# Second block on an unscaled residual, gates as token rows, scan sums by accumulating transfers, a one-matmul bucket row, aligned buffers

## What is computed

```python
h = rms_norm_2(x, norm_w)
q, k, v, a_gate, u, z, g_a, g_s = split(h @ w_in)
attn = sliding_window_attention(rms(q), rms(k), v, sinks)
y_a = (attn * silu(a_gate)) @ w_attn_proj
y_ssm = gelu(s5_ssm(u, ...))          # s[t] = a * s[t-1] + b[t], complex, 4096 states
glu_a, glu_b = split(y_ssm @ w_glu + b_glu)
y_s = (glu_a * sigmoid(glu_b) * silu(z)) @ w_ssm_proj
merged = sigmoid(g_a) * y_a + sigmoid(g_s) * y_s
out = x + merged @ w_out
```

## Time and profile before

| | us |
|---|---|
| median of three runs | 3322.17 |
| profiled execution, its own time | 3322.21 |
| its span, first to last instruction | 3320.3 |
| PE busy / PEld busy | 3140.2 / 2725.1 |
| DVE busy / ACT busy / POOL busy | 2021.3 / 1538.3 / 59.3 |
| mean granted clock | 0.983 |

### The profile page before, as it was taken

How to read it: one execution, slowest core, us unless ns; L and a number is a source line. 1 busy time by engine, 2 the same in 40 slices (tenths; PEclk the granted TensorE clock), 3 DMA queues, 4 the chain that set the end, 5 groups by cost and what they waited for, 6 DMA issues and landing times.

```text
span 3320.3 us, 47412 instructions
## 1 busy us (share of the span) xinstructions
PE 3140.2 (95%) x17370; PEld 2725.1 (82%) x17370; DVE 2021.3 (61%) x2350; ACT 1538.3 (46%) x1975; POOL 59.3 (2%) x99
## 2 busy tenths in 40 slices
PE   8999898999999998989989999999997998999999
PEld 7798777888888887987877888888885888989997
DVE  5567755555555555676655555555556557888664
ACT  5554545544444444545455444444444455544443
POOL 0000000000000000000000000000001000000000
PEclk9999999999999999999999999999998999999999
DMA  6645363655555555544554555555553433444555
GB/s 238 221 167 175 134 211 119 207 189 188 190 187 189 187 189 171 178 147 152 180 169 154 196 184 190 189 190 189 184 189 114 164 111 129 156 146 153 169 178 180
DMA packets 159835, 577.01 MB, mean 174 GB/s; under 512 B 17504, under 2 KB 20240, under 8 KB 158544
## 3 DMA queue, kind: packets, MB, share of 16 engines
q1 hardware_dynamic: 151936, 549.52, 49.6%
q10 hardware_dynamic: 5616, 13.51, 1.2%
q0 software_dynamic: 2144, 12.02, 1.0%
HBM read 568.43 MB, written 6.55 MB: 173 GB/s over the span
## 4 chain that ended last, share of the span: by engine, by line
PE 74%; DVE 11%; ACT 5%; issue 4%; DVEq 3%; DMA 1%; ACTq 1%; POOL 1%; POOLq 0%; SPq 0%
PE acc L624 19%; PE acc L626 19%; PE acc L625 19%; PE acc L632 4%; PE acc L634 4%; PE acc L635 4%; DVE lo L1482 3%; PE tp L643 1%; DVE sr L2098 1%; ACT hi L1020 1%; PE tp L676 1%; ACT lg L1102 1%; DVEq L2076 0%; PE tp L774 0%; ACT ze L1353 0%
## 5 line engine op out<-in xcount | busy, mean ns | idle before, releaser
L1482 DVE TENSOR_TENSOR lo<-raw,hi 128x1024 fp32r<-128x1024 f32 x1040 | 1263.4, 1223 | 943.5 <-ACT hi L1020 934.7
L1020 ACT ACTIVATE hi<-raw 128x1024 fp32r<-128x1024 f32 x1040 | 1093.9, 1058 | 1273.6 <-PE acc L626 970.4
L624 PE MATMUL acc<-hi,xh 128*128 128x512 f32 (+2 forms) x2272 | 883.8, 389 | 6.7 <-DVE lo L1482 3.7
L625 PE MATMUL acc<-lo,xh 128*128 128x512 f32 (+2 forms) x2272 | 875.8, 385 | 0.0
L626 PE MATMUL acc<-hi,xl 128*128 128x512 f32 (+2 forms) x2272 | 875.5, 385 | 0.0
L632 PE MATMUL acc<-xh,hi 128*128 128x256 f32 x1664 | 487.3, 293 | 35.9 <-DVE lo L1482 35.5
L624 PEld LDWEIGHTS acc<-hi,xh 128*128 128x128 f32 x2272 | 428.5, 189 | 94.7 <-issue 6.6
L626 PEld LDWEIGHTS acc<-hi,xl 128*128 128x128 f32 x2272 | 428.4, 189 | 85.1
L625 PEld LDWEIGHTS acc<-lo,xh 128*128 128x128 f32 x2272 | 428.7, 189 | 82.5
L634 PE MATMUL acc<-xl,hi 128*128 128x256 f32 x1664 | 476.3, 286 | 0.0
L635 PE MATMUL acc<-xh,lo 128*128 128x256 f32 x1664 | 476.0, 286 | 0.0
(11 more groups left out here) (366 smaller groups left out, 2629.8 us busy)
## 6 DMA issues: line engine op xcount, KB each, us to landing
raw<-in_stream SPq DMA_DIRECT2D x1040, 512.0 KB, 3.4
gpost<-in_post_g POOLq DMA_DIRECT2D x6, 1024.0 KB, 5.1
bpad<-in_b_pad ACTq DMA_DIRECT2D x8, 512.0 KB, 5.1
row<-in_rows POOLq DMA_DIRECT2D x3, 896.0 KB, 8.7
toep_scratch<-toep ACTq DMA_DIRECT2D x1, 2304.0 KB, 7.9
y<-in_mem SPq DMA_DIRECT2D x4, 512.0 KB, 8.4
h<-in_x ACTq DMA_DIRECT2D x4, 512.0 KB, 5.8
mem_scratch<-memkv ACTq DMA_DIRECT2D x1, 2048.0 KB, 6.6
```

Of the source, the lines that this page charges most:

```text
L624: nc.tensor.matmul(o, ah, hi[s][:, k, 0:g.width], start=first, stop=False)
L625: nc.tensor.matmul(o, ah, lo[s][:, k, 0:g.width], start=False, stop=False)
L1020: nc.scalar.activation(hi[s][:, :, :], raw[s][:, :, :], ACT.Copy).then_inc(hi_done, 1)
L1482: nc.vector.tensor_tensor(lo[s][:, :, :], raw[s][:, :, :], hi[s][:, :, :].bitcast(F32), ALU.subtract).then_inc(split_done, 1)
```

## The change

- **Bucket row.** One matmul (`relt` as weights, 12 rows by 384) is done before the first product; ACT copies the 12x384 result and one transfer writes it to memory 128 times over. The six turns in mem_k1 are gone. The second and the fourth transposes of the memory rows move ahead, ACT's and DVE's splits of unit 0 stand ahead of the first `xh`, and a one-column copy by ACT stands first of all. The step-size arithmetic of DVE and the keys of the second layer change places.
- **Aligned buffers.** `sb` starts at a multiple of 512 and rounds sizes to 64, so that every buffer starts on a multiple of 64 bytes.
- **Unscaled residual in the second block.** `raw_norm` takes the place of `norm`. q, kv and the gates are scaled by `rs` as ACT reads them; u, ag and z by `rsb2` (the row of `rs` on all partitions) as DVE reads them, with ACT's Silu after it on SBUF.
- **Token rows.** ga, ap, gs and sp are in form T (96 units). The merged rows stand in `y`, and PE transposes them in four turns `mix0` to `mix3` before the groups out.
- **Scan sums.** `back` and `forward` no longer add: DVE writes the four products of each into `sds` and `srs`, and POOL issues a transfer of 128x2048 elements that adds `srs` to `sds` (two in a pass). `join` is gone, `scan` waits for the first sum and moves to position 3.2, `forward` to 4.1; PE's `outputs` waits for the second.
- The second block's part of the parameters is no longer loaded at the end of layer 2.

```diff
@@ groups, steps
-    SECOND += [(f"ga{_n}", KD, W, "C"), (f"ap{_n}", 8, W, "C")]
+    SECOND += [(f"ga{_n}", KD, W, "T"), (f"ap{_n}", 8, W, "T")]
...
-        scan = [(0, "inputs", c), (1, "back", c), (2, "maps", c), (2.8, "scan", c), (4, "forward", c), (5, "join", c),
+        scan = [(0, "inputs", c), (1, "back", c), (2, "maps", c), (3.2, "scan", c), (4.1, "forward", c),
                 (7.2, "outputs", c), (7.9, "skip", c)]
@@ buffers
-        place = [nc.sbuf_base + (-nc.sbuf_base) % 64]
+        place = [nc.sbuf_base + (-nc.sbuf_base) % 512]
...
-            place[0] += (int(np.prod(shape[1:])) * 4 + 31) // 32 * 32
+            place[0] += (int(np.prod(shape[1:])) * 4 + 63) // 64 * 64
@@ PE
             mem_quad(0)
+            mem_quad(1)
+            pe.wait_ge(start_loaded, 32)
+            pe.wait_ge(acc_read[1], 1)
+            nc.tensor.matmul(acc[1][0:12, 0, 0:TOEP], relt[:, :], oneh[:, :], start=True, stop=True).then_inc(toep_full, 1)
...
-                if 1 <= n <= 6:
-                    if n == 1:
-                        pe.wait_ge(rel_spread, 1)
-                    o = flat(take_turn(pe, pos, MTP[f"toep{n - 1}"]))
-                    for m in range(2):
-                        last = nc.tensor.matmul(o[:, m * W:m * W + TOEP], relb[:, 2 * (n - 1) + m, :], oneh[:, :],
-                                                start=True, stop=True)
-                    last.then_inc(tp_full, 1)
...
-            ready = norm(pos, 0, "norm", STP)
-            product(pos, SG["q0"], xh, xl, quad_ready=ready)
+            ready = raw_norm(pos, 0, "norm", STP)
+            product(pos, SG["q0"], xh, xl, unit_ready=ready)
             product(pos, SG["q1"], xh, xl)
+            pe.wait_ge(rs_spread, pos.n(1, 1))
+            for t in range(NT):
+                transposes(pos, STP[f"rsb{t}"], [(0, 0, rs_wide2[:, t, :])])
...
-                    pe.wait_ge(states, c + 1)
+                    pe.wait_ge(states, 16 * (c + 1))
...
+            def mix_quad(q):
+                pe.wait_ge(merged_done, q + 1)
+                transposes(pos, STP[f"mix{q}"], [(c, t, y[:, t, (4 * q + c) * P:(4 * q + c + 1) * P])
+                                                 for c in range(4) for t in range(NT)])
             for n in range(4):
                 product(pos, SG[f"sp{n}"], prh, prl)
+                if n:
+                    mix_quad(n - 1)
@@ ACT
+                if q == 3:
+                    act.wait_ge(toep_full, 1)
+                    nc.scalar.activation(toep[:, :], acc[1][0:12, 0, 0:TOEP], ACT.Copy).then_inc(toep_copied, 1)
...
+            act.dma_start(toep_scratch.rearrange("(p h w) -> h p w", h=12, w=TOEP),
+                          toep[:, :].unsqueeze(1).to_broadcast([12, P, TOEP])).then_inc(toep_moved, 16)
...
+            def scaled_out(name, out, func=ACT.Copy):
+                g = SG[name]
+                ahead(name)
+                a = see_group(act, pos, g)
+                for t in range(NT):
+                    last = nc.scalar.activation(out[:, t, :], a[:, t, :], func, scale=rs[:, t:t + 1])
+                last.then_inc(acc_read[g.parity], 1)
@@ DVE
+            def by_rows(name, out):
+                g = SG[name]
+                a = see_group(dve, pos, g)
+                return nc.vector.tensor_tensor(out, a[:, :, :], rsb2[:, :].unsqueeze(1).to_broadcast([P, 4, T]),
+                                               ALU.mult).then_inc(acc_read[g.parity], 1)
...
-                    nc.vector.tensor_tensor(sr[0][:, :, :], o[:, :, :], rots[:, :, :], ALU.mult)\
+                    nc.vector.scalar_tensor_tensor(sr[1][:, :, :], o[:, :, :], -1.0, rots[:, :, :], ALU.mult, ALU.mult)\
...
-                    nc.vector.tensor_tensor(sd[0][:, :, :], sd[0][:, :, :], st[:, :, :], ALU.add)
-                    nc.vector.tensor_tensor(sd[1][:, :, :], sd[1][:, :, :], sr[0][:, :, :], ALU.subtract)
+                    dve.drain().then_inc(backed, 1)
...
-                    dve.drain()
+                    dve.wait_ge(summed, 16 * (c + 1))
...
-                elif step == "join":
-                    c = at[0]
-                    dve.drain()
-                    nc.vector.tensor_tensor(sd[0][:, :, :], sd[0][:, :, :], st[:, :, :], ALU.subtract)
-                    nc.vector.tensor_tensor(sd[1][:, :, :], sd[1][:, :, :], sr[1][:, :, :], ALU.add).then_inc(states, 1)
+                    dve.drain().then_inc(turned_back, 1)
@@ POOL
+            for c in range(NCT):
+                hold(pool, backed, c + 1, passed)
+                pool.dma_start(flat(sds), flat(srs), accum_op=ALU.add).then_inc(summed, 16)
+                hold(pool, turned_back, c + 1, passed)
+                pool.dma_start(flat(sds), flat(srs), accum_op=ALU.add).then_inc(states, 16)
```

More of the change, by code:

```diff
@@ L293, in build @@
         mixT = at_offset("mixT", y_at, [P, KD, T])
+        par_at = place[0]
         par = sb("par", [P, NPC])
@@ L1163, in _ @@
             act.dma_start(bias[:, 11, :], shifted[:, 11 * TOEP:11 * TOEP + T]).then_inc(toep_moved, 16)
+            units.before(pos, MG["mem_k1"], 3, MU)
             act.wait_ge(ssm_ready, 1)
@@ L1619, in _ @@
                     mem_keys(0)
-            units.ahead(pos, MG["mem_k1"], MU)
+            units.before(pos, MG["mem_k1"], 1, MU)
             dve.wait_ge(ssm_exp, 1)
@@ L1645, in _ @@
             dve.drain()
-            units.before(pos, MG["mem_v1"], 3, MU)
+            units.before(pos, MG["mem_k1"], 5, MU)
             dve.wait_ge(ssm_exp, 2)
@@ L1667, in _ @@
             dve.drain()
+            units.ahead(pos, MG["mem_k1"], MU)
+            mem_keys(1)
             dve.wait_ge(x_loaded, 64)
@@ L1950, in _ @@
             dve.wait_ge(par2_loaded, 16)
[L1951 to L1955 removed]
+            raw_norm(pos, 0, "norm", STP, lambda c: spar[:, SC["norm_w"].start + c:SC["norm_w"].start + c + 1], SG["q0"],
+                     add=True)
+            units.before(pos, SG["q0"], 7, SU)
+            dve.wait_ge(in_roots, pos.n("norm", NT))
+            nc.vector.tensor_copy(rs_wide2[:, :, :], rs.unsqueeze(2).to_broadcast([P, NT, P])).then_inc(rs_spread, 1)
             for m in range(2):
```

201 lines of the change are left out of this document (115 added, 86 removed).

## The result

The changed kernel takes 3333.18 us (median of 12 runs, 3329.01 to 3342.05), beside 3322.69 for the kernel before in the same comparison: ratio 1.0035, 95% interval 1.0027 to 1.0044. It is slower by 0.35%: 10.5 us between the medians, 11.6 by the ratio. The forecast was 3294, faster than before. The profiled execution has a span of 3335.0 us (before 3320.3).

The account below looks back on a forecast made before the run. The prediction took PE's matmuls as the bound (74% of the chain), with DVE's chain adding 4.8 us to each scan pass. Its terms summed to -28.3 against 3322.21, giving 3293.9, stated as 3294, range 3250 to 3335.

Parts of the forecast that it names:

- start: Start of the kernel, bucket row: six turns and the stall at 109.59 go, the early write costs stream time; -12.2 us.
- alignment: Products fed by `hTh` or `cqh`: each unit gains 0.09 us if 32 bytes off alignment is the cause; -17.2 us.
- norm: Entry of the second block: takes the time of layer 2's unscaled entry, 22.46 us instead of 36.2; -13.8 us.
- form T behind the scan, transposes: PE: 29 units behind the scan gain 0.16 us each, -4.6; added transposes cost +4.0.
- readings by `rsb2`: Second block: six products read by DVE, 7.3 us of its time, a third of it counted; +2.5 us.
- scan sums: Scan: POOL's adding transfers make a pass 45.9 us instead of 44.2, over 7.5 passes; +13 us.
- T: Scan: time from the end of DVE's four products to the landing of POOL's adding transfer; taken as 7.4 us.
- Rival D: Products from `hTh`: alignment does nothing, its 0.09 us has another cause; +17, 3311 us; chance 0.13.
- 31.1 + 2T: Scan: length of a pass in us, as long as that is over what PE needs; 45.9 forecast.
- Rival C: Scan: slow transfer eats all other gains at T = 9.3, slower beyond, 3348 us at T = 11; chance 0.17.

Follow-up runs that it names:

- old_places: The changed kernel with the buffer placing of the kernel before (start a multiple of 64, sizes rounded to 32): ratio 1.0047.
- read_by_act: sums_dve with u, ag and z read by ACT as before and DVE's multiplication by `rsb2` left out: ratio 0.9939.
- sums_dve: The changed kernel with the four sums of a pass given back to DVE: ratio 0.9982, 3314.12 us.
- before_places: The kernel before with only its buffers moved, so xh, hTh, gath, prh, cqh stand a multiple of 512 bytes from hi: ratio 0.9941.
- plain_copy: The changed kernel with POOL's two transfers of a pass as plain copies, the sums left out: ratio 0.9924.
- best2: sums_dve with hTh, gath, prh a multiple of 512 from hi, the bucket row's 18 KB stored once and spread by POOL from memory to memory: ratio 0.9913.
- start_places: before_places with the start of best2, second block as in the kernel before: ratio 0.991, 3289.79 us.

## Why the prediction was wrong, by its own steps

| term | forecast | measured | from |
|---|---|---|---|
| start | -12.2 | -4.5 | the 104th split |
| alignment | -17.2 | -4 | old_places against the changed kernel |
| norm | -13.8 | -14.4 | splits 824 to 858 |
| form T behind the scan, transposes | -0.6 | +0.8 | splits 988 to the end |
| readings by `rsb2` | +2.5 | +14 | read_by_act against sums_dve |
| scan sums | +13 | +17.6 | the changed kernel against sums_dve |
| sum | -28.3 | +9.5 | |

The sum of the right column is close to the measured difference of the medians, 10.5 us. But its rows are of different kinds. Start, norm and form T are read from one execution of each kernel. For the 4 of alignment the two intervals overlap. And how the loss in the scan is shared between readings and sums depends on the order in which they are taken out. Together they were forecast at 15.5 and are 31.6 by the table, 35 by the passes (48.9 for 44.2, 7.5 times) and 37.5 by the splits, the largest miss of all.

The measured time, 3333, lies inside the stated range of 3250 to 3335, at the end that was meant for a T near 10. With T at 9.2 that is luck: the other gains had to shrink as well.

*Alignment* failed by 13 us, as "If it is the 32 bytes that separate 2.81 from 2.72". The pair of rows was read rightly (the buffer's place does it, worth 20 us in all on the kernel before, as before_places shows), but two buffers can't tell a start's remainder by 64 from its distance to `hi`, and I took the one that the edit was about. The changed `hTh` is aligned to 64 and as slow. Rival D said so in effect, with a wrong reason: "comes from something else about that product". No row of the trace before could have told the two in form T: `cqh`, the third buffer there, is 32 bytes off 64 and 480 from `hi`, and slow too. The changed kernel's `cqh` and `hTh` tell them. The Trainium skill, "SBUF — State Buffer", section "Operand start alignment", asks for a multiple of the element only; these runs show a cost beyond that, of 5 to 7 ns a start.

*Readings* failed as "a third is taken" of DVE's busy time. With the sums on DVE they cost 14, and the upper end of 7.3 was too low as well. The chain ACT reads, DVE uses became DVE multiplies, ACT waits, DVE uses, and ACT in order holds back the splits. The prediction asked what is queued behind DVE's wait for the transfer and not what is queued behind ACT's wait for DVE. That this wait makes the 14 is argued: plain_copy has the same readings and such waits, and loses nothing in the scan against before.

*Start* failed in the write. I took 6.7 us of stream for 2.3 MB at 348 GB/s and half of it; in pieces of 1.5 KB from 12 partitions it held the weights 21.5 us and PE 10.8. The wait at 109.59 did go, and so did the six turns. The first product, from which 2.4 us were taken, came no earlier: it starts at 13.30, for 13.02 before, because the second transposes of the memory rows now stand ahead of it and wait 2.14 for their load. With the other write, best2's 13.7 at the 104th split is more than the 12.2 forecast.

*Scan sums*: the mechanism was right and the size off, and this is the step that turned the sign. T was 7.4 and is 9.2: 0.6 from DVE's end to POOL's issue, for which the prediction had nothing, and 8.6 to the landing. What was mis-sized besides is "I count the part that grows with size twice": 2.8 + 2 x 2.3 made 7.4 of it, and the sum takes 8.6, where the copy takes 5.3. The formula 31.1 + 2T gives 49.5 with it, measured 48.9, and for plain_copy (T = 5.9) 42.9, measured 43.6; both without any term for the readings. So in the changed kernel itself T alone is enough for the loss in the scan: a pass is longer than before's 44.2 by 5.3 by the formula and by 4.7 measured, 7.5 times. The 17.6 of the table is less because it compares with a pass of 46.6, in which DVE has both the sums and the readings. No run has the changed kernel without its readings.

The slope was 1.6 a pass and not 2. The formula also has no term for PE's slow restarts, which the start's sum did have. After a wait of 3.12 us in the second pass the starts are 0.43 apart again, and the granted clock from 2810 to 2815 us is 0.50:

```profile
2809.79 0.79 PE L638 MATMUL acc<-hi,xh 128*128 128x512 f32 x1 [3.12 <-DVE lo L1528]
2810.38 0.63 PE L639 MATMUL acc<-lo,xh 128*128 128x512 f32 x1
2810.81 0.63 PE L640 MATMUL acc<-hi,xl 128*128 128x512 f32 x1
```

Over the scan the mean granted clock is 0.93 in the changed kernel, 0.96 in sums_dve and 0.97 before and in plain_copy. How much of the loss is wait and how much slow restart, no run separates.

Rival C's point, T = 9.3, was all but reached; the kernel came out slower at 9.2 because the gains set against it were 41 forecast and some 22 real.

## What to carry to other kernels

Where an edit turns "engine A reads the result" into "B reads, A goes on with it", look at A's wait and what A's queue holds back, not only at B's busy time; here the readings cost 14 us where DVE had the sums too, twice their busy time. A transfer may do an engine's addition, but only up to the bytes whose landing that engine can fill with work of its own: half a sum beside DVE gained 16 us on start_places (on best2 nothing), whole sums lost 18. When one buffer is slower than another at the same work, list the addresses of all operands, in both kernels, before believing a rule about one of them.
